# A hybrid block on Trainium2: the next delta head's decays clipped in the scan, and two modulation pairs of the opening on VectorE

## The reference

```python
mod = jnp.split(silu(c) @ w_mod + b_mod, 9)            # the same for c_ctx
h = _rmsnorm(x, pre_g) * (1.0 + scale) + shift         # the opening
a, b = jnp.split(h @ w_gu, 2, axis=-1)                 # first feed-forward

# delta rule, per head and chunk; gcum = cumsum of the log decays g
decay = exp(where(lower_incl, gcum[i] - gcum[j], -inf))
l_mat = where(strict, (kb @ k.T) * decay, 0.0)
u, w  = solve_unit_lower(l_mat, [v * beta, kb * exp(gcum)])
intra = where(lower_incl, (q @ k.T) * decay, 0.0)
v_new = u - w @ s                                      # scan over the chunks
o = (q * exp(gcum)) @ s + intra @ v_new
s = s * exp(gcum[-1]) + (k * exp(gcum[-1] - gcum)).T @ v_new
```

## Time and profile before

| | |
|---|---|
| median of 3 runs | 2095.82 us |
| the profiled execution | 2089.0 us, span 2087.3 us |
| mean granted clock of TensorE | 0.985 |
| TensorE busy | 2005.8 us (96%) |
| VectorE busy | 1126.4 us (54%) |
| ScalarE busy | 797.7 us (38%) |
| GpSimd busy | 225.4 us (11%) |
| moved by DMA | 174.73 MB |

### The profile page before, as it was taken

How to read it: one execution, slowest core, us unless ns; L and a number is a source line. 1 busy time by engine, 2 the same in 40 slices (tenths; PEclk the granted TensorE clock), 3 DMA queues, 4 the chain that set the end, 5 groups by cost and what they waited for, 6 DMA issues and landing times.

```text
span 2087.3 us, 31229 instructions
## 1 busy us (share of the span) xinstructions
PE 2005.8 (96%) x11329; PEld 1714.1 (82%) x11329; DVE 1126.4 (54%) x2027; ACT 797.7 (38%) x1291; POOL 225.4 (11%) x211
## 2 busy tenths in 40 slices
PE   8999999999996999999999999999999979999996
PEld 4788888888884779888988888898888858888885
DVE  2677655555456655476676667666533353233335
ACT  4322222111236555465456536544422352223122
POOL 0000000000000210041342144133000000000000
PEclk9999999999998999999999999999999999999998
DMA  8233333333221330011011001100222413222322
GB/s 310 88 119 118 119 123 122 128 121 123 79 81 68 116 92 1 11 46 46 30 45 45 33 33 45 45 29 22 71 98 93 141 40 102 100 97 95 101 91 80
DMA packets 49035, 174.73 MB, mean 84 GB/s; under 512 B 6724, under 2 KB 6852, under 8 KB 48720
## 3 DMA queue, kind: packets, MB, share of 16 engines
q1 hardware_dynamic: 37632, 129.95, 18.4%
q0 software_dynamic: 11344, 43.97, 6.3%
HBM read 167.03 MB, written 4.24 MB: 82 GB/s over the span
## 4 chain that ended last, share of the span: by engine, by line
PE 86%; issue 5%; ACT 4%; DVE 4%; POOL 1%; DMA 0%; ACTq 0%; DVEq 0%; SPq 0%; POOLq 0%
PE ps L1370 79%; PE ps L1374 4%; PE ps L1608 1%; DVE d_w L1226 1%; ACT w_hi L411 1%; DVE X L894 1%; DVE n_y L886 1%; PE ps L1737 1%; POOL d_s L370 1%; DVE w_lo L812 0%; ACT L699 0%; ACT L694 0%; ACT d_qd L693 0%; ACT d_c L696 0%; DMA X<-XT 0%
## 5 line engine op out<-in xcount | busy, mean ns | idle before, releaser
L1370 PE MATMUL ps<-h_hi,w_hi 128*128 128x512 f32 (+1 forms) x1712 | 547.4, 369 | 16.7 <-DVE h_lo L869 10.9
L411 ACT ACTIVATE w_hi<-raw 128x1024 fp32r<-128x1024 f32 x221 | 233.8, 1058 | 794.5 <-PE ps L1370 794.5
L1370 PE MATMUL ps<-h_lo,w_hi 128*128 128x512 f32 (+1 forms) x1712 | 536.3, 360 | 0.0
L1370 PE MATMUL ps<-h_hi,w_lo 128*128 128x512 f32 (+1 forms) x1712 | 528.6, 358 | 0.0
L812 DVE TENSOR_TENSOR w_lo<-raw,w_hi 128x1024 fp32r<-128x1024 f32 x221 | 272.2, 1232 | 437.8 <-ACT w_hi L411 437.6
L1370 PEld LDWEIGHTS ps<-h_hi,w_hi 128*128 128x128 f32 x1712 | 318.8, 189 | 72.5 <-issue 22.9
L1370 PEld LDWEIGHTS ps<-h_lo,w_hi 128*128 128x128 f32 x1712 | 323.4, 189 | 49.1 <-issue 3.4
L1370 PEld LDWEIGHTS ps<-h_hi,w_lo 128*128 128x128 f32 x1712 | 323.6, 189 | 48.5
L1370 PE MATMUL ps<-g_hi,w_hi 128*128 128x512 f32 (+1 forms) x528 | 158.4, 355 | 0.0
L1370 PE MATMUL ps<-g_lo,w_hi 128*128 128x512 f32 (+1 forms) x528 | 157.9, 354 | 0.0
L1370 PE MATMUL ps<-g_hi,w_lo 128*128 128x512 f32 (+1 forms) x528 | 157.9, 354 | 0.0
(11 more groups left out here) (264 smaller groups left out, 2687.3 us busy)
## 6 DMA issues: line engine op xcount, KB each, us to landing
raw<-W SPq DMA_DIRECT2D x221, 512.0 KB, 3.4
w_mod<-WMOD POOLq DMA_DIRECT2D x56, 512.0 KB, 3.7
w_mod<-WMOD SPq DMA_DIRECT2D x16, 512.0 KB, 14.2
g_row<-g_rows POOLq DMA_DIRECT2D x8, 768.0 KB, 6.2
X<-XT SPq DMA_DIRECT2D x4, 768.0 KB, 7.4
a_sw<-i_n POOLq DMA_DIRECT2D x40, 64.0 KB, 1.9
x_spill<-X POOLq DMA_DIRECT2D x1, 2048.0 KB, 7.7
X<-x_spill POOLq DMA_DIRECT2D x1, 2048.0 KB, 8.4
```

What stands on the lines that cost most here:

```text
L411: a.activation(w_hi[:, b.pair], raw[:, b.raw], ACT.Copy).then_inc(s("w_hi"), 1)
L1370: return pe.matmul(out, lhsT, rhs, start=start, stop=stop)
```

## The change

Two sets of edits.

In the delta heads the difference is written to `d_t[:, d]` itself, and `decay_clip` makes `d_r` from it and then clips it in place. The first difference comes ahead of the masks, with the split of block b[3] behind it; the second stays after mask 2. The first clip stands behind the split ahead of the scan, the second behind the first residual. The three taps of the next head's query convolution move from steps 0 to 2 of the scan, behind the new state, to steps 2 to 4, ahead of it. The split of block b[2] moves from ahead of the decays to behind `d_l`. ScalarE's four exponentials move from the levels into the scan, behind the `d_vn` copies of steps 1 to 4.

In the opening pairs 6 and 7 are multiplied on VectorE: 16 quarters `mod0_part` of four instructions, three ahead of the first splits, one behind the first `n_t`, and three behind each `h_lo` of k = 0 to 3; TensorE only sums them over the partitions. Each of the eight pairs has a place of its own (pairs 0 and 1 where parts of `h_hi` and `h_lo` come later), so SP waits for none; the order of loads is pairs 0 and 6, weight blocks 0 and 1, pairs 1, 7, 2, 3, 4, 5. The squares have four places, VectorE adds them in pairs, and TensorE sums four times and not eight.

```diff
@@ -53,6 +53,8 @@
 MOD0_PAIRS = 6
+MOD0_ORDER = [0, 6, 1, 7, 2, 3, 4, 5]
+DVE_MOD0 = 6
 LEVELS = 7
@@ -124,13 +126,15 @@
         w_mod0 = at("w_mod0", 148, [MOD0_PAIRS, 2, KT, P])
+        w_first = [at("w_first0", 48, [2, KT, P]), at("w_first1", 72, [2, KT, P])]
         m_part = at("m_part", 203, [4, 2, P])
         m_one = at("m_one", 203, [4, P])
-        m0_row = at("m0_row", 196, [2, 2 * P])
+        m0_part = at("m0_part", 196, [4, 2, P])
+        m0_row = at("m0_row", 200, [2, 2 * P])
         y_acc = at("y_acc", 95.5, [T])
...
         n_sq = at("n_sq", 124, [2, T])
-        n_acc = at("n_acc", 130, [T])
+        n_each = at("n_each", 136, [4, T])
         n_rs = at("n_rs", 133, [T])
@@ -228,6 +232,10 @@
 
+        def mod0_at(k):
+
+            return w_first[k] if k < 2 else w_mod0[:, k - 2]
+
         def cols(t_all, t_x, i, k, lo, hi):
@@ -265,20 +273,23 @@
             XTv = XT.rearrange("(k p) t -> p k t", p=P)
-            def load_mod(k):
-                for i in range(2):
-                    sp.dma_start(w_mod0[:, k % MOD0_PAIRS, i].rearrange("p k n -> p (k n)"), WMOD[k + KT * i])\
+            def load_mod(i):
+                k = MOD0_ORDER[i]
+                for u in range(2):
+                    sp.dma_start(mod0_at(k)[:, u].rearrange("p k n -> p (k n)"), WMOD[k + KT * u])\
                       .then_inc(s(f"mod0_loaded{k}"), 16)
...
                     sp.dma_start(ca[:], CA).then_inc(s("ca_loaded"), 16)
+            load_mod(0)
+            load_mod(1)
             for b in range(2):
                 sp.dma_start(raw[:, b], Wv[b]).then_inc(w_loaded[b], 16)
-            for k in range(KT):
-                if k >= MOD0_PAIRS:
-                    sp.wait_ge(s("mod_row"), k - MOD0_PAIRS + 1)
-                load_mod(k)
+            for i in range(2, MOD0_PAIRS):
+                load_mod(i)
+            for i in range(MOD0_PAIRS, KT):
+                load_mod(i)
             for b in range(2, RING):
@@ -424,13 +435,16 @@
                 for k in range(KT):
-                    if q or k >= 2:
+                    if q:
                         a.wait_ge(s("sq_used"), KT * q + k - 1)
+                    elif k >= 4:
+                        a.wait_ge(s("sq_pair"), k // 2 - 1)
                     if r == 0 and k % 2 == 0:
...
                         a.wait_ge(s("x_new"), ready + k + 1)
-                    a.activation(n_sq[:, k % 2, lo:T], src(k), ACT.Square).then_inc(s("sq_ready"), 1)
+                    sq = n_sq[:, k % 2, lo:T] if q else n_each[:, k % 4, :]
+                    a.activation(sq, src(k), ACT.Square).then_inc(s("sq_ready"), 1)
 
@@ -461,7 +475,7 @@
                 for k in range(KT):
-                    if r == 0 and k + 1 < KT:
+                    if r == 0 and k + 1 < DVE_MOD0:
                         mod_row(k + 1)
@@ -657,11 +671,11 @@
             def decay(h, d):
+                a.wait_ge(s("d_mn"), h * 4 + (2 * d + 2))
+                a.activation(d_t[:, d], d_t[:, d], ACT.Exp).then_inc(s("d_e1"), 1)
+
+            def decay_out(h, d):
                 a.wait_ge(s("d_mn"), h * 4 + (2 * d + 1))
-                a.activation(d_t[:, d], d_t[:, d], ACT.Exp).then_inc(s("d_e1"), 1)
-
-            def decay_out(h, d):
-                a.wait_ge(s("d_mn"), h * 4 + (2 * d + 2))
                 a.activation(d_r[:, d, 0:NC_X], d_r[:, d, 0:NC_X], ACT.Exp, scale=-1.0).then_inc(s("d_e2"), 1)
@@ -722,12 +736,12 @@
                         scaled(i)
-                    if not final and i in (6, 7, 12, 13):
-                        (decay if i % 2 == 0 else decay_out)(h + 1, (i - 6) // 6)
                 for t in range(NCH):
...
                         a.activation(d_vn[:, d, t % 2], ps[:, 4 + d, P:2 * P], ACT.Copy, scale=-1.0 if t else 1.0).then_inc(s("sc_n"), 1)
+                    if not final and t in (1, 2, 3, 4):
+                        (decay if t % 2 else decay_out)(h + 1, (t - 1) // 2)
                 if not final:
@@ -747,8 +761,8 @@
             for d in range(2):
+                decay_out(0, d)
                 decay(0, d)
-                decay_out(0, d)
             take(first[1])
@@ -974,6 +988,32 @@
             v.tensor_scalar(small[:, 16:24], vec[:, V_BMOD + KT:V_BMOD + 2 * KT], 1.0, None, ALU.add).then_inc(s("bias1"), 1)
+            for j in range(KT // 2):
+                v.wait_ge(s("sq_ready"), 2 * j + 2)
+                if j >= 2:
+                    v.wait_ge(s("sq_used"), 2 * j - 2)
+                v.tensor_tensor(n_sq[:, j % 2], n_each[:, 2 * j % 4], n_each[:, 2 * j % 4 + 1], ALU.add).then_inc(s("sq_pair"), 1)
+
+            def mod0_part(n):
+                u, part = n // 4, n % 4
+                k = DVE_MOD0 + u // 2
+                if n % 8 == 0:
+                    v.wait_ge(s(f"mod0_loaded{k}"), 32)
+                for kk in range(2 * part, 2 * part + 2):
+                    for c in range(2):
+                        acc, w = m0_part[:, u, c, :], mod0_at(k)[:, u % 2, kk, :]
+                        if kk == 0:
+                            x = v.tensor_scalar(acc, w, silc[:, kk, c:c + 1], None, ALU.mult)
+                        else:
+                            v.wait_ge(s("mod0_acc"), 14 * u + 2 * kk + c - 1)
+                            x = v.scalar_tensor_tensor(acc, w, silc[:, kk, c:c + 1], acc, ALU.mult, ALU.add)
+                        if kk < KT - 1:
+                            x.then_inc(s("mod0_acc"), 1)
+                if n % 8 == 7:
+                    x.then_inc(s("mod0_part"), 1)
+            v.wait_ge(s("silc"), 1)
+            for n in range(3):
+                mod0_part(n)
             split(Blk(0, 0, 0))
@@ -986,6 +1026,7 @@
             scaled(0)
+            mod0_part(3)
             for k in range(KT):
@@ -994,6 +1035,8 @@
                 low(k)
+                for n in range(4 + 3 * k, min(4 + 3 * k + 3, 16)):
+                    mod0_part(n)
             ffn(0, B_FFN1, segs_all, False, 0)
@@ -1177,19 +1220,16 @@
                     v.wait_ge(s("d_row"), h * 16 + 16)
-                else:
-                    v.wait_ge(s("d_mn"), h * 4 + 2)
-                v.tensor_tensor(d_q[:, 1], hn[:, G_GC + 6 * d:G_GC + 6 * d + 6].unsqueeze(2).to_broadcast([P, NCH, P]),
+                v.tensor_tensor(d_t[:, d], hn[:, G_GC + 6 * d:G_GC + 6 * d + 6].unsqueeze(2).to_broadcast([P, NCH, P]),
                                 g_row[:, d], ALU.subtract).then_inc(s("d_diff"), 1)
 
-            def decay_min(h, d):
+            def decay_clip(h, d):
                 v.wait_ge(s("d_diff"), h * 2 + (d + 1))
-                v.tensor_scalar(d_t[:, d], d_q[:, 1], 0.0, None, ALU.min).then_inc(s("d_mn"), 1)
-
-            def decay_max(d):
-                v.scalar_tensor_tensor(d_r[:, d, 0:NC_X], d_q[:, 1, NC_CTX:], 0.0,
+                v.scalar_tensor_tensor(d_r[:, d, 0:NC_X], d_t[:, d, NC_CTX:], 0.0,
                                        no_tri[:, d, :].unsqueeze(1).to_broadcast([P, NC_X, P]), ALU.max, ALU.add)\
                  .then_inc(s("d_mn"), 1)
+                v.wait_ge(s("d_mn"), h * 4 + (2 * d + 1))
+                v.tensor_scalar(d_t[:, d], d_t[:, d], 0.0, None, ALU.min).then_inc(s("d_mn"), 1)
 
@@ -1198,7 +1238,6 @@
                 v.tensor_tensor(d_c[:, 0, CTX + 2:], d_c[:, 0, CTX + 2:], d_rs[:, 0:SEQ], ALU.mult).then_inc(s("d_qk"), 1)
-                step(b[2])
                 v.wait_ge(s("d_e1"), h * 2 + 1)
@@ -1212,6 +1251,7 @@
                  .then_inc(s("d_l"), 1)
+                step(b[2])
                 v.wait_ge(s("d_l"), h + 1)
@@ -1236,18 +1276,12 @@
                     tables_next(h + 1)
+                    decay_diff(h + 1, 0)
+                step(b[3])
                 for i in range(18):
                     masked(i)
-                    if i == 7:
-                        step(b[3])
-                    if final:
-                        continue
-                    if i in (2, 9):
-                        decay_diff(h + 1, i // 9)
-                    if i in (4, 11):
-                        decay_min(h + 1, i // 11)
-                    if i in (5, 12):
-                        decay_max(i // 12)
+                    if i == 2 and not final:
+                        decay_diff(h + 1, 1)
                 for gr in range(3):
@@ -1256,7 +1290,7 @@
                     step(Blk(B_DN, h, 4))
-                    v.wait_ge(s("d_qd"), h * 2 + 2)
+                    decay_clip(h + 1, 0)
                 def residual(t):
@@ -1277,10 +1311,14 @@
                         residual(t)
+                    if not final and t == 1:
+                        decay_clip(h + 1, 1)
+                    if not final and t in (2, 3, 4):
+                        if t == 2:
+                            v.wait_ge(s("d_qd"), h * 2 + 2)
+                        conv_tap(h + 1, 0, t - 2)
                     if t < NCH - 1:
                         new_state(t)
-                    if t < 3 and not final:
-                        conv_tap(h + 1, 0, t)
                 if not final:
```

(28 more changed lines are left out.)

## The result

After the change the kernel takes 2098.61 us (median of 14 runs, 2095.47 to 2108.89), before 2097.0 in the same job: ratio 1.0037, 95% interval 1.0021 to 1.0053 (it is not the quotient of the two medians, which is 1.0008). That is a little slower. The forecast was 2096.7, in a range of 2082 to 2106.

What follows compares the result with a forecast made beforehand. TensorE was taken to bound the kernel, with 86% of the chain of waits. Terms -10.6 + 11.9 + 1.5 - 2.8 + 0.9 = +0.9 us on the median 2095.82 gave 2096.7, in a range of 2082 to 2106.

Steps and rivals of the forecast that it cites:

- rival C: Delta heads: TensorE's clock falls after 2.0 us idle before its first product; +12.6 in all, 2104 to 2109; chance 0.22.
- Stalls gone, 1.5 us a head: Mask phase of seven heads: TensorE sets the pace at all levels, gaining 1.5 us x 7 = 10.6.
- The first mask late by 1.70: Ahead of the masks: difference and split wait for GpSimd, so the first mask starts 1.70 us later; +11.9 over seven heads.
- Rivals A: Ahead of the first mask: VectorE runs the split right behind the difference; 0.78 late for 1.70; 2090.3; chance 0.27.
- B: Ahead of the first mask: nothing is blocked, heads gain their 1.5 in full; 2084.2; chance 0.20.
- The scan, -0.4 a head: Scan: with the taps moved, TensorE's wait for `d_rhs` goes; -0.4 x 7 = -2.8 us (0 to -4).
- both clips fitting by 0.1: Scan: both clips fit VectorE's idle times by 0.1 us; if either is late by 0.3 it costs 2.
- The clock in the heads: Delta heads: no clock fall in the sum; as a rival, 1.8 a head lost, +12.6 in all, chance 0.22.
- The last head, +1.5: Last head: the split ahead of its first mask costs 1.7, less 0.2 from the mask phase; +1.5 us.
- The opening, +0.9: Opening: VectorE's quarters replace two TensorE products, -0.3, and one clock fall costs 1.2; +0.9 us (-0.4 to +3).
- the late fall: Opening: TensorE idles between units, its clock falls once, and columns come about 1.2 us after VectorE wants them.
- The load: Opening: pair 1, now the fourth megabyte, lands at 23.2 us, setting the first columns at 26.8, against 26.62 before.

Runs made afterwards that it cites:

- the kernel with GpSimd held: The changed kernel with GpSimd's second level waiting until VectorE has made the first mask; 2077.31 us, ratio 0.9944.
- the gap filled: The changed kernel with 16 unread products of zeros on TensorE ahead of the first level in all eight heads; 2086.25 us, ratio 0.9967.
- the opening alone: The kernel before with only the change's edits of the opening; 2090.37 us, ratio 0.9993.
- the heads alone: The kernel before with only the change's edits of the delta heads; 2100.50 us, ratio 1.0022.

## Why the prediction was right, and what was not

The time, 2098.6, lies 1.9 above the forecast, well within the range. But it is made of other parts than the forecast's sum: rival C, given 0.22, is what happened in the heads. Step by step:

- **Stalls gone, 1.5 us a head**: right. Masks come each 1.34 us, and a head without a fall in the clock has the whole of it.
- **The first mask late by 1.70**: right in place and price. The difference was to end at 986.9, GpSimd's product to go first, the split to end at 988.97 and the mask to start at 988.9; it started at 988.78. TensorE's idleness grew by 1.74 (0.34 to 2.08). Rivals A (0.78) and B (0) fall by this row, and the kernel with GpSimd held shows what B would have been: 71.5 us a head.
- **The scan, -0.4 a head, both clips fitting by 0.1**: right: -0.42, with 0.20 and 0.19 to spare.
- **Together**, a head without a fall was to be 0.2 shorter than before, 73.2. The one in the change took 73.19, the seven with the gap filled 73.19 to 73.23.
- **The clock in the heads, left out of the sum**: this is the step that failed. The forecast put 0 for it and kept it as a rival, because the only fall in the rows of before came after 2.22 us of idleness and this would be 2.0. It fell with 2.08, in six heads of seven. The price worked out for it, 1.8 a head, was high: 1.3 to 1.6 measured (the other heads less 73.19), 8.9 us in all. The trace of before held a second fall that the forecast overlooked: its last head starts the levels at 0.50 after idle times of only 0.93, 1.43 and 0.51 us.
- **The last head, +1.5**: too high. The split made its mask late by 1.80 as said (4.92 us behind the head's mark, before 3.12), but the levels of this head began at half clock before the change too, and the full clock came back a level earlier now. The last level's product was 0.6 late (29.45 us behind the mark against 28.86).
- **The opening, +0.9**: +0.93 in the profile of the change, but that is luck twice over. Over the five profiles of this opening it is +2.4, and +2.0 by the time of the opening alone, so the term was too small by over 1 us: the late fall was priced at 1.2 and mostly costs more. And in the profile of the change two errors cancel. The forecast had one fall of the clock; there were two. The 2.47 us of waiting for pair 1 brought its product from 3.62 to 5.30, so that the first columns came at 28.05 and not 26.8. In return a unit without a quarter takes VectorE 3.5 us (54.98 to 58.48), not 3.61, and a quarter 1.02 (28.69 to 54.98 less four such units, by twelve), not 1.07. The columns that came late behind the other fall cost 1.17 here, as priced. The load stood about where it was put: pair 1's product started at 22.8, forecast 23.2.

From rows that is: heads -1.5 and +8.9, last head +0.4 (from its mark to the span's end), opening +0.9, in sum +8.7. The lower groups differ by 8.5, the upper by 9.8, the two profiled spans by 6.5. The rest of the latter lies between 73 and 905 us, where nothing is changed and where one profile differs from another by up to 3 us. The ratio, 1.0037 or 7.8 us, has all of these within its interval.

So the nearness of the number is in part luck. The change adds 8 to 10 us, the forecast added 0.9; but it added them to a median of three runs of which two were of the upper group, and the median of the 14 runs after lies in the lower.

## What to carry to other kernels

Before moving VectorE work with two SBUF inputs into an idle gap, lay GpSimd's instructions beside the gap, add the whole length of each one it meets, and let the one that has waited go next; if GpSimd's work isn't urgent, hold that instead (one wait was worth 3.0 us a head here, 74.5 to 71.5). Then ask what the added idleness does to the engine that waits: 1.7 us more of it cost TensorE 1.3 to 1.6 more in clock, wherever the clock fell. A price that decides the sign belongs in the sum at its chance, not beside it.

## What the runs showed that was not expected

- The same idleness brings the clock down in one head and not in another: of fourteen heads with 2.00 to 2.10 us in front (the change and the heads alone), eleven fell, to 0.57 to 0.72 over 4 us, and three did not. Those with 0.35 us never did, in 63 heads of nine kernels. It is not chance from head to head, though. Read in steps of 0.5 us, the clock of the change falls 0.1 us ahead of the first product in the first head, 0.5, 1.0, 1.4 and 1.7 behind it in the next four, not at all in the sixth, and 0.4 behind it in the seventh. In the heads alone it is not at all, 1.5, 1.7, not at all, 0.5, 1.0 and 1.4. So its moment moves on steadily and then drops out; what it goes by, no run shows.
- The first wait of the opening does the same: after 2.46 to 2.48 us of idleness the clock fell in five profiles and not in a sixth (the opening alone, 2.46: the product took 3.61 us, not 5.30).
- Three short idle times close together, 0.93, 1.43 and 0.53 us, were followed by a clock of 0.62, as a single one of 2.08 was. All eight kernels that have them in the last head show it, with 0.50 to 0.64.
